# Powers of a block-diagonal matrix as 32 columns on four tile places, and a gram moved behind the fourth doubling

## What is computed

```python
def step(S, inp):
    r_t, w_t, k_t, v_t, z_t, b_t = inp
    s_z = jnp.einsum('ghvk,ghk->ghv', S, z_t)
    S = S * w_t[:, :, None, :] + s_z[..., None] * b_t[:, :, None, :] + v_t[..., None] * k_t[:, :, None, :]
    return S, jnp.einsum('ghvk,ghk->ghv', S, r_t)
_, y = lax.scan(step, jnp.zeros((G, H, dh, dh), jnp.float32), (r, w, k, v, z, b))
```

## Time and profile before

| | us |
|---|---|
| median of 3 runs | 2987.35 (2986.55 to 2989.48) |
| the profiled execution | 2980.72, its span 2978.5 |
| recurrence, layer 0 | about 125 |
| recurrence, layer 1 | about 121 |
| PE busy | 2771.8 (93%) |

### The profile page before, as it was taken

One profiled execution on the slowest core, in us unless ns is written; L12 is line 12 of the kernel. 1 busy time (PEld: TensorE's weight loads), 2 busy tenths in 40 slices (PEclk: granted clock), 3 DMA queues, 4 the chain that ended last, 5 costly groups with the idle time before them and its releaser, 6 DMA issues.

```text
span 2978.5 us, 50806 instructions
## 1 busy us (share of the span) xinstructions
PE 2771.8 (93%) x21394; PEld 2323.2 (78%) x21394; DVE 1932.2 (65%) x2283; ACT 1482.3 (50%) x1757; POOL 64.7 (2%) x44
## 2 busy tenths in 40 slices
PE   6997879999989978789999999999999889998999
PEld 4874766888768768768788787887877779996999
DVE  3355855222453657468888888888887557665665
ACT  3344233212333432357776677767776445454443
POOL 1100000000002000010000000000000000000000
PEclk9998999999999989889999999999999989998999
DMA  7514101222225230069999898989996424541453
GB/s 310 219 57 187 50 2 57 102 96 99 98 73 198 72 149 4 2 270 371 335 366 338 337 365 334 373 336 348 365 347 254 160 99 170 187 157 72 156 184 114
DMA packets 81460, 581.70 MB, mean 195 GB/s; under 512 B 9064, under 2 KB 10736, under 8 KB 11504
## 3 DMA queue, kind: packets, MB, share of 16 engines
q1 hardware_dynamic: 78192, 571.49, 50.9%
q10 hardware_dynamic: 3072, 7.33, 0.7%
HBM read 577.73 MB, written 1.05 MB: 194 GB/s over the span
## 4 chain that ended last, share of the span: by engine, by line
PE 81%; DVE 8%; PEld 4%; ACT 3%; issue 2%; DMA 1%; PEldq 0%; DVEq 0%; ACTq 0%; POOLq 0%; POOL 0%; SPq 0%
PE banks L2404 20%; PE banks L2428 10%; PE banks L2731 9%; PE banks L1028 8%; PE banks L816 8%; PE banks L1054 4%; PE banks L850 3%; PE banks L1471 3%; PE banks L3049 3%; PEld banks L644 2%; PEld banks L1983 2%; DVE ring_split L2581 1%; PE banks L488 1%; DVE x_buf L2570 1%; PE banks L2757 1%
## 5 line engine op out<-in xcount | busy, mean ns | idle before, releaser
L2581 DVE TENSOR_TENSOR ring_split<-ring,arena_split 128x2048 fp32r<-128x2048 f32 x336 | 768.2, 2291 | 91.4 <-ACT arena_split L2509 82.5
L2509 ACT ACTIVATE arena_split<-ring 128x2048 fp32r<-128x2048 f32 x336 | 644.2, 1918 | 52.9 <-PE banks L2428 52.9
L306 DVE TENSOR_TENSOR ring_split<-ring,arena_split 128x2048 fp32r<-128x2048 f32 x144 | 329.8, 2292 | 343.7 <-ACT arena_split L300 343.7
L300 ACT ACTIVATE arena_split<-ring 128x2048 fp32r<-128x2048 f32 x144 | 274.3, 1908 | 101.6 <-PE banks L1028 74.0
L2404 PE MATMUL banks<-arena_split 128*128 128x512 f32 x896 | 300.8, 398 | 11.6 <-DVE ring_split L2581 11.6
L2404 PE MATMUL banks<-arena_split,mix_split 128*128 128x512 f32 x896 | 303.2, 401 | 6.4 <-DVE ring_split L2581 6.4
L2428 PE MATMUL banks<-arena_split 128*128 128x512 f32 x896 | 297.4, 392 | 1.0 <-DVE arena_split L2610 1.0
L2404 PEld LDWEIGHTS banks<-arena_split 128*128 128x128 f32 x896 | 169.0, 189 | 48.9 <-DVE ring_split L2581 13.4
L2404 PEld LDWEIGHTS banks<-arena_split,mix_split 128*128 128x128 f32 x896 | 168.4, 188 | 45.2 <-DVE ring_split L2581 8.3
L2428 PEld LDWEIGHTS banks<-arena_split 128*128 128x128 f32 x896 | 168.2, 188 | 43.5 <-issue 4.4
L816 PE MATMUL banks<-mix_split,ring_split 128*128 128x256 f32 x704 | 199.1, 283 | 0.0
(11 more groups left out here) (392 smaller groups left out, 5478.0 us busy)
## 6 DMA issues: line engine op xcount, KB each, us to landing
ring<-parts SPq DMA_DIRECT2D x541, 1024.0 KB, 4.8
arena<-bias ACTq DMA_DIRECT2D x2, 2048.0 KB, 9.1
x_buf<-xt SPq DMA_DIRECT2D x1, 2048.0 KB, 13.0
constants<-con SPq DMA_DIRECT2D x1, 2026.0 KB, 8.2
out<-x_buf ACTq DMA_DIRECT2D x1, 1024.0 KB, 4.9
arena<-lora ACTq DMA_DIRECT2D x2, 256.0 KB, 3.2
arena<-gate ACTq DMA_DIRECT2D x2, 256.0 KB, 3.5
arena<-sgw ACTq DMA_DIRECT2D x2, 256.0 KB
```

The costliest lines, as they stand in the source:

```text
L300: act.activation(high[:, m % depth, :], slots[:, n % RING, :], ACT.Copy).then_inc(w_high.h, w_high.one(times))
L306: dve.tensor_tensor(low_slots[:, n % RING, :], slots[:, n % RING, :], high[:, m % high.shape[1], :].bitcast(F32), ALU.subtract).then_inc(w ...
L2509: act.activation(high[:, m % 3, :], slots[:, m % RING, :], ACT.Copy).then_inc(wh_ok.h, 1)
L2581: dve.tensor_tensor(low_slots[:, m % RING, :], slots[:, m % RING, :], high[:, m % 3, :].bitcast(F32), ALU.subtract).then_inc(wl_ok.h, 1)
```

## The change

The diagonal blocks of D, its powers and E are kept in 32 columns and not in 64: of each 64x64 item only the two 32x32 blocks on the diagonal are held, 8 x 32 = 256 columns in place of 512. A product of two such matrices (`block_products`) is 32 matmuls of 32x32 on the four places (0,0), (32,32), (64,64), (96,96) in turn, in place of 16 of 64x64 on two. Both D and D^T are now made by `block_grams`, 32 matmuls each (64 rows, 32 columns, 32 wide), in place of the masks over `dl` and the z half of `zb`; `zb` keeps its r half and goes away in the two unused steps. The full gram `dl` stands behind the fourth doubling `p4`, and LL is made behind e4. The first coupling product (`to_blocks`) is 32 matmuls that put two halves into two banks; the second is 32 matmuls with 64 columns. `solve_blocks` is 16 matmuls in place of 8. `p6`, `p7`, `solve`, `state`, `outputs`, the keys and the transposes stay. The evictions of D, D^T, the powers and E have 256 columns.

```diff
 for _name, _n in [("mean_d", 128), ("head_sum", 128), ("ident", 128), ("eye64", 64), ("mask_zr", 512),
-                  ("mask_d", 256), ("mask_l", 256), ("mask_dt", 256), ("not_first", 512), ("swap", 128),
+                  ("mask_d", 128), ("mask_l", 256), ("mask_dt", 128), ("eye32", 32), ("not_first", 512), ("swap", 128),
...
-    put("mask_dt", np.concatenate(two(fwd_st * same, bwd_st * same), 1))
-    put("mask_d", np.concatenate(two(bwd_st * same, fwd_st * same), 1))
+    row_in, col_in = row % 32, np.arange(32)[None, :]
+    near = (row_in // 16 == col_in // 16) * 1.0
+    above, under = (row_in < col_in) * near, (row_in > col_in) * near
+    put("mask_dt", np.concatenate(two(above, under), 1))
+    put("mask_d", np.concatenate(two(under, above), 1))
+    put("eye32", (p[:, None] % 32 == np.arange(32)[None, :]) * 1.0)
...
-        DT, DD, LL, D2, D2T, BS, KS, VS, GG_ = (take() for _ in range(9))
-        E = [take() for _ in range(2)]
+        BK = 32
+        take_blocks = lambda: gb.take(8 * BK, 8)
+        DT, DD, D2, D2T = (take_blocks() for _ in range(4))
+        N1, LL, BS, KS, VS, GG_ = (take() for _ in range(6))
+        E = [take_blocks() for _ in range(2)]
...
-        D4, N1, D4T, D8 = DT, DT, DD, D2T
+        D4, D4T, D8 = DT, DD, D2T
+        blocks_in = lambda i: v3(bank(i)[:, 0:256], 8)
...
+            def block_products(out, left, right):
+                for i in range(8):
+                    for at in range(0, P, BK):
+                        r = slice(at, at + BK)
+                        mm = pe.matmul(out[r, i, :], left[r, i, :], right[r, i, :], start=True, stop=True,
+                                       tile_position=(at, at))
+                return mm
+            def to_blocks(left, right):
+                for i in range(8):
+                    for k in range(2):
+                        for h in hs:
+                            at = first_row(h) + k * BK
+                            mm = pe.matmul(bank(k)[h, i * BK:(i + 1) * BK], left[at:at + BK, i, :], right[at:at + BK, i, :],
+                                           start=True, stop=True, tile_position=(at, first_row(h)))
+                return mm
+            def block_grams(g, part, left_of, right_of):
+                for j in range(2):
+                    for hp, d, q in items():
+                        c, o = CHUNKS[d][2 * g + j], part + (2 * j + hp) * BK
+                        for k in range(2):
+                            for h in hs:
+                                at = first_row(time_half(h, q)) + k * BK
+                                mm = pe.matmul(bank(d)[at:at + BK, o:o + BK], left_of(h, q, c, k), right_of(h, q, c, k),
+                                               start=True, stop=True, tile_position=(first_row(h), at))
+                return mm
...
-            def against_zr(keys, g, j):
+            def against_zr(keys, g, j, lo=0):
                 rows = 2 if seen(g) else 1
                 for hp, d, q in items():
                     c, at = CHUNKS[d][2 * g + j], (2 * j + hp) * P
-                    z_r = zr[:, q, c, 0:rows, :].rearrange("p w t -> p (w t)")
+                    z_r = zr[:, q, c, lo:rows, :].rearrange("p w t -> p (w t)")
                     for h in hs:
-                        mm = pe.matmul(bank(3 + d)[time_half(h, q), at:at + rows * CH], keys[h, q, c * CH:(c + 1) * CH], z_r[h],
+                        mm = pe.matmul(bank(3 + d)[time_half(h, q), at + lo * CH:at + rows * CH], keys[h, q, c * CH:(c + 1) * CH], z_r[h],
                                        start=True, stop=True)
...
-            def apply(name, region, left, s, j):
-                for hp, d, q in items():
-                    for h in hs:
-                        mm = pe.matmul(bank(5 + d)[h, spot(d, region, hp)], left[h, 4 * j + q, :], RH[h, q, :], start=True, stop=True)
-                mm.then_inc(P_.h, P_.one(f"{name}{j}_{s}"))
             def solve_blocks(s, j):
                 pe.wait_ge(V_.h, V_.at(f"e4_{s}"))
                 pe.wait_ge(A_.h, A_.at(f"rhs{j}_{s}"))
-                apply("w", BLOCKS, E[s % 2], s, j)
+                for hp, d, q in items():
+                    for at in range(0, P, BK):
+                        r = slice(at, at + BK)
+                        mm = pe.matmul(bank(5 + d)[r, spot(d, BLOCKS, hp)], E[s % 2][r, 4 * j + q, :], RH[r, q, :],
+                                       start=True, stop=True, tile_position=(at, at))
+                mm.then_inc(P_.h, P_.one(f"w{j}_{s}"))
...
+                z_in = lambda h, q, c, k: zr[h, q, c, 0, k * BK:(k + 1) * BK]
+                b_in = lambda h, q, c, k: bt[h, q, c * CH + k * BK:c * CH + (k + 1) * BK]
                 if g:
                     pe.wait_ge(A_.h, A_.at(f"bs_{s}"))
+                block_grams(g, 0, z_in, b_in)
+                block_grams(g, P, b_in, z_in).then_inc(P_.h, P_.one(f"dc_{g}"))
+                if g:
+                    pe.wait_ge(V_.h, V_.at(f"g_{s}"))
+                    pe.wait_ge(A_.h, A_.at(f"vs_{s}"))
+                if seen(g):
+                    against_zr(bt, g, 0, 1)
+                    against_zr(bt, g, 1, 1).then_inc(P_.h, P_.one(f"zb_{g}"))
+                if g:
+                    rhs(s, 0)
+                fill_pe(pe, g, "zb")
+                pe.wait_ge(V_.h, V_.at(f"dt_{g}"))
+                block_products(blocks_in(2), DD, DT)
+                block_products(blocks_in(0), DT, DD).then_inc(P_.h, P_.one(f"p1_{g}"))
+                if g:
+                    solve_blocks(s, 0)
+                pe.wait_ge(V_.h, V_.at(f"mb1_{g}" if seen(g) else f"e1_{g}"))
+                against_zr(kt, g, 0).then_inc(P_.h, P_.one(f"kb0_{g}"))
+                fill_pe(pe, g, "p1")
+                pe.wait_ge(V_.h, V_.at(f"d2_{g}"))
+                pe.wait_ge(A_.h, A_.at(f"d2t_{g}"))
+                block_products(blocks_in(0), D2T, D2)
+                block_products(blocks_in(1), D2, D2T)
+                block_products(blocks_in(2), D2, E[g % 2]).then_inc(P_.h, P_.one(f"p2_{g}"))
...
+                fill_pe(pe, g, "p3")
+                pe.wait_ge(V_.h, V_.at(f"e3_{g}"))
+                pe.wait_ge(A_.h, A_.at(f"d8_{g}"))
+                block_products(blocks_in(2), D8, E[g % 2]).then_inc(P_.h, P_.one(f"p4_{g}"))
...
-                against_zr(bt, g, 0)
-                against_zr(bt, g, 1).then_inc(P_.h, P_.one(f"zb_{g}"))
...
-                products(b8(2), DD, DT)
-                pe.wait_ge(V_.h, V_.at(f"l_{g}"))
-                products(b8(1), DT, DD).then_inc(P_.h, P_.one(f"p1_{g}"))
...
                     pe.wait_ge(V_.h, V_.at(f"km1_{g}"))
                     outputs(s, 0)
                     rhs(s, 1)
                 fill_pe(pe, g, "p4")
-                pe.wait_ge(V_.h, V_.at(f"e4_{g}"))
-                products(b8(0), LL, E[g % 2])
-                products(b8(1), E[g % 2], LL).then_inc(P_.h, P_.one(f"p5_{g}"))
+                pe.wait_ge(V_.h, V_.at(f"l_{g}"))
+                to_blocks(LL, E[g % 2])
+                block_products(b8(2), E[g % 2], LL).then_inc(P_.h, P_.one(f"p5_{g}"))
...
-                after(f"dl_{g}")
-                mult(dirs(DD), grams, wide("mask_d"), f"d_{g}")
-                after(f"zb_{g}")
-                for d in range(2):
-                    mult(of_dir(DT, d), zr_of(d)[:, :, :, 0, :], per_dir(mdt, d), f"dt{d}_{g}")
-                mult(dirs(LL), grams, wide("mask_l"), f"l_{g}")
+                after(f"dc_{g}")
+                mult(dirs(DD), block_grams(0), wide("mask_d", 2 * BK), f"d_{g}")
+                mult(dirs(DT), block_grams(P), wide("mask_dt", 2 * BK), f"dt_{g}")
                 own()
-                add(e, DT, eye, f"e1_{g}")
+                add(e, DT, block_eye, f"e1_{g}")
                 if seen(g):
+                    after(f"zb_{g}")
                     for d in range(2):
                         mult(of_dir(MB[g % 2], d), zr_of(d)[:, :, :, 1, :], per_dir(mzr[:, :, 1, :], d), f"mb{d}_{g}")
                 after(f"p1_{g}")
-                copy(D2, b8(1), f"d2_{g}")
+                copy(D2, blocks_in(0), f"d2_{g}")
                 after(f"kb0_{g}")
                 keys_out(g, 0, rows)
                 taps.some(dve, 1)
                 after(f"p2_{g}")
-                copy(D4, b8(0), f"d4_{g}")
-                add(e, b8(2), e, f"e2_{g}")
+                copy(D4, blocks_in(0), f"d4_{g}")
+                add(e, blocks_in(2), e, f"e2_{g}")
                 after(f"kb1_{g}")
                 keys_out(g, 1, rows)
                 taps.some(dve, 1)
                 after(f"p3_{g}")
                 own()
-                add(e, b8(1), e, f"e3_{g}")
+                add(e, blocks_in(1), e, f"e3_{g}")
                 if g:
                     state(s, 0)
                 taps.some(dve, 1)
                 after(f"p4_{g}")
                 own()
-                add(e, b8(2), e, f"e4_{g}")
+                add(e, blocks_in(2), e, f"e4_{g}")
+                after(f"dl_{g}")
```

(6 more changed lines are left out.)

81 lines of the change are left out of this document (34 added, 47 removed).

## The result

The changed kernel takes 3093.3 us (median of 4 runs, 3088.05 to 3100.35) against 2986.95 us (4 runs, 2984.5 to 2989.48) for the kernel before beside it: 1.0357 times as long, with an interval of 1.0335 to 1.0380, or 106 us more. The forecast was 3067 with a range of 3042 to 3100. The sign, the mechanism and the range held; the sum was 26 us short.

A forecast was written before the change was run, and what follows sets the result against it. PE was taken to be bound in the recurrences by its instruction supply, in blocks of 256: 105.9 us for added packets, less 31.1 of slack, plus 5, gives +80 us on the median, 3067 us, range 3042 to 3100.

The forecast's parts named there:

- The bound: In both recurrences, PE is limited by the supply of instructions in blocks of 256; chance 0.84.
- The number of packets: Over both recurrences, 7,552 more PE instructions: 15.0 packets more in layer 0 and 14.5 in layer 1, 156 becoming about 185.
- the first: Recurrences: packets start earlier when instructions are used faster, so steps get 3 us shorter: 2963 us; chance 0.06.
- the second: Recurrences: supply keeps up, but no record takes under 15.2 ns, so +2 us a step: 3003 us; chance 0.06.
- The third: Block products: the four places write one bank and don't run together, 30 ns a record, +115 us: 3102 us; chance 0.04.
- the 7.6 that I took: Products on four places with 32 columns: 7.6 ns per record, between bounds of 7.6 and 15.2, hidden behind the supply.
- the shortest mean cycle: Time per 256 PE instructions in the recurrences: 3.48 us in layer 0, 3.70 in layer 1; +105.9 us for the added packets.
- The slack: Spare time in dense stretches (8.2 and 4.5 us) and first steps (7.9 and 10.5): -31.1 us, with +5 us given back.
- The 9 us that I had in the upper end for a lower clock: Upper end of the range only: 9 us for a lower granted clock, within a sum of +113 us.
- The evictions: D, D^T, powers and sum at 256 columns: DVE 0.69 to 0.42 us, ACT 0.60 to 0.38, worth nothing behind late blocks.
- the moved gram: Off-diagonal gram behind the fourth doubling: 0.4 us a step, 3 us in all if not covered by late blocks; counted zero.
- The changes of tile shape: 13 changes a step, at most 1.5 us a step and 12 us in all; zero in the sum, 5 us at the upper end.

The follow-up runs named there:

- wide: The change with the same instruction count, but 28 of the 32 matmuls of each doubling product moving 64 columns instead of 32: 3089.4 us.
- pairs: The change with half the doubling matmuls, each twice as wide, same columns moved (products of odd items are other numbers): 3033.5 us.
- repad: The change with two unused gaps in the table of constants, so all buffers lie at the addresses of the kernel before: 3082.6 us.
- after_again: The changed kernel itself, unaltered, run once more on the same chip as the kernel with the gaps in the table of constants: 3094.6 us.
- back: The change with the full gram back at the head of the step and the wait for L inside the first doubling, same instructions: 3092.8 us.
- plus64: The kernel before with the 64 block-gram matmuls added once a step, into columns that nobody reads: 3012.1 us.
- eights: The change with only item 0's four matmuls per doubling product, 256 columns each (other items' numbers differ), 157 instruction packets: 3002.3 us.
- eights_back: eights with the full gram back at the head of the step and the wait for L inside the first doubling: 3009.8 us.
- merged_before: The kernel before with the two products with left side D2 in the second doubling merged into one of 128 columns: 2983.0 us.
- plus128: The kernel before with the 64 block-gram matmuls added twice a step, into columns that nobody reads: 3052.4 us.
- eights_repad: eights with the two gaps in the table of constants, so all buffers lie where they lie in the kernel before: 2991.6 us.
- merged_after: The change with the two products with left side D2 in the second doubling merged into one of 64 columns: 3077.9 us.

## Why the prediction was right, and what it mis-sized

**The bound: right.** The three stops of the earlier trace rows were the tip of it. That 1,776 records and their bare waits are 7 x 256 gave the block, and the distance between packet and resumption gave the cycle. wide and pairs show that the count of instructions sets the time of the change, and not the array. One sign was off: the packets were to come every 3.4 to 3.8 us and the steps to take 34 to 38 us. The means are 3.97 and 3.88 us, and from gram to gram the steps take 37.5, 37.3 and 41.9 us in layer 0 and 32.5, 34.3 and 37.9 in layer 1.

**The number of packets: exact.** 29 forecast, 29 measured. Of the rivals, the first and the second (the supply keeps up) fall with the 62 stops at block edges, and by 130 and 90 us. The third (the four places don't run together) gave 3102 us, close to the measured time, so the time alone would not have told it from the supply. wide and the timeline do. Were the places slow enough to fill the steps, 1,792 matmuls of twice the width could not be free. And the 64 records of the fourth doubling that start at 1207.77 come every (1.07 - 0.22)/63 = 13.5 ns, at a clock of 0.50 (between 1207.5 and 1209.0), where the third rival had 30 at the full one:

```profile
1207.50:1209.00 1.50, 1.50 (x76) 0.50 0.04 11
...
1207.77 1.07 PE L1489 MATMUL banks<-arena 32*32 32x32 f32 x64
```

At a clock of 1.00 the mean distance was 8.9 ns, near the 7.6 that I took. The Trainium skill's "TensorEngine Tiling (Array Packing)", section "Gotcha 1: PSUM Pressure", by which the third rival would be the result, does not agree with this trace.

**Layer 0: a price that was too small and a slack that was not there.** I took the shortest mean cycle, 1.15 + 1.05 + 1.28 = 3.48 us, from blocks of a kernel that mostly did not wait for them. Measured over 36 packets it was 3.97 us. 36 x (3.97 - 3.48) = 18 us, and layer 0 is that much over the forecast: 56 us (54.6 in repad and after_again, 50.2 in wide, 48.2 in back) where 52.2 - 8.2 - 7.9 + 2.5 = 38.6 were due. A slower packet is not the reason: it took 1.9% of 16 x 142.8 us / 36 = 1.21 us and not 1.05 in the change, but 1.7% of 16 x 142 us / 36 = 1.07 us in repad, whose layer 0 is hardly cheaper.

About half of the 18 us lies in the first step. From its first gram to that of the second step it took 24.4 us before and 37.5 with the change: 13.2 us for 3.5 packets more, where 3.5 x 3.48 - 7.9 + 0.6 = 4.9 were due. The earlier trace rows have a DMA share of 0.53 for this step, and the prediction passed over it ("DMA is at 1 to 2% of its capacity there"). The stretch of the change (length; PE busy and records; clock; DMA; GB/s) and PE's timeline:

```profile
296.80:303.00 6.20, 2.41 (x195) 1.00 1.01 424
...
303.07 1.50 PE L1489 MATMUL banks<-arena 32*32 32x32 f32 x93 [3.59 <-issue]
```

The weights fill the DMA engines. PE goes into a block at 297.40, and the next instruction packet starts at 300.60, 3.2 us later, where it is 0.6 to 1.9 us in the later steps. PE stands for 3.59 us inside the first doubling. Every kernel here with added or smaller matmuls has this one stop: 1.0 us in plus64, 2.3 to 5.1 in the others, 2.3 and 2.4 in eights and eights_repad. before and merged_before have none. So the slack of 7.9 us in this step was not to be had.

In layer 1 the recurrence took 41.5 us more, as forecast (53.7 - 4.5 - 10.5 + 2.5 = 41.2), but by luck of two errors. Its first step took 32.5 us and not 27.0, 5.5 more for 3.25 packets, where 3.25 x 3.70 - 10.5 + 0.6 = 2.1 were due; the later steps came out 3 us under. The prediction had the dearer cycle in its range ("with 3.9 us everywhere"), and should have taken it as the likeliest: the kernel before already ran at 3.87 and 3.94 us on average, and a cycle is never shortest each time.

**The slack: of the right kind.** plus64 cost 25.7 us where 8 x 3.9 = 31 would have been the full price, and pairs 33.5 us inside the recurrences for 13 packets, where 51 would have been. So the first packets find about 5 to 17 us of slack, where the sum took off 31 and gave back 5. These times don't tell a smaller slack from a dearer packet, and the 18 us below stand for both.

**The addresses: the term that was missing.** The sum had nothing for code that the change does not touch, and gave no reason for that. I read the three changed widths in the table of constants as a matter of masks, and did not ask what lies behind them in memory. That is the 12 us between the change and repad. The 9 us that I had in the upper end for a lower clock covered it by luck.

**The sum, mended:** 80 us, 18 for layer 0 and 12 for the addresses make 110, against 106 measured. Of the 120 us between the two profiled executions some 6 belong to the one of before, which was 6.6 us under the median of its runs, and 7 to that of the change, which was 7 us over its median. So parts read from them hold to a few us only. The 6 us that repad still takes more behind layer 1 are the same in merged_before (6.0) and plus128 (5.8), so the changed form as such does not bring them; what does is open.

**The evictions and the moved gram: right, worth nothing.** The evictions had the forecast sizes, and back shows the gram's place to be free in the change. eights_repad adds that shorter products and evictions together bring nothing even without added blocks, which I had left open. The changes of tile shape, 5 us at the upper end, were not tested by themselves.

## What to carry to other kernels

Before small matmuls are cut into smaller ones, count PE's instructions against time: an fp32 matmul is four of them here, and in these recurrences PE waited for its program where 256 instructions would have taken less than about 3.9 us, whatever the tile places could do. There fewer matmuls made the change faster (pairs by 60 us, merged_after by about 15), and twice the columns at the same count cost nothing (wide). Look at the DMA share too: where the weights filled the DMA engines, the next block came later still. A stop "<-issue" inside a run of equal matmuls is the sign to look for; divide the instructions between two such stops by 256. And here a change of one table moved all that is allocated behind it: where a small part of a kernel is changed, keep the other addresses as they were, or the comparison holds something else as well.

## What was unexpected of the hardware

- The place of the buffers in memory changed the time of matmuls that read them: 392 against 395 ns on average (128 columns, 512 moving) for an arena 896 bytes lower, 12 us over the whole kernel. Which part of the address matters is open, and so is whether the read alone is slower or meets the other engines' accesses.
- With the DMA engines filled by weights (424 GB/s from 296.8 to 303.0 us) the next instruction packet started 3.2 us after PE had gone into its block, and PE stood for 3.59 us.
- A 16 KB instruction packet took 1.21 us on average in the dense part of layer 0 with the change, 1.07 in repad and 1.05 us before (1.20 in layer 1 before), single ones from 0.88 to 1.5. In the change, wide and back, whose programs are of one length, the long ones sat at other places each time, so they don't belong to a place in the program.
- The Trainium skill, "Runtime: NRT & Kernel Launch", section "Instruction fetch mechanics", gives PE room for 2,048 instructions. In the dense part of layer 0 of the change (330 to 445 us) a packet started 0.6 to 1.9 us after PE had gone into a new block, and never two of them for one block: the trace shows PE one block ahead at most, not eight.
- The granted clock went to and fro between its two levels inside the changed recurrences (means of 0.78 and 0.73, against 0.99 and 0.93 before), and was higher in wide (0.91 and 0.87), which moves more columns in the same time. It cost little there: the recurrences of wide took 175.3 and 162.5 us, those of the change 181.3 and 162.4.
